# A three-layer block on one core: first attention ordered by token tile, its values held stationary on two column strips, and three conditioning pieces weighed by GpSimd

## The reference

```
# layer_ab (first attention)
y = rms_norm(x, norm_g) @ w_in            # split into qa ka va qi ki wi za qb kb vb zb
oa = attention A: 8 heads of 64, 2 key/value heads, keys chosen by an index score (top 64)
ob = attention B: 8 heads of 64, 2 key/value heads, window of 128 tokens, a sink per head
mix = concatenate([oa * silu(za), ob * silu(zb)])
x = x + mix @ w_out                        # 1024 x 1024
# layer_cd starts with
y = rms_norm(x, norm_g) @ w_in
# conditioning of the third layer: 12 pieces of 512 columns
mod = silu(c) @ w_ada + b_ada              # one row for all tokens
```

## Time and profile before

| | us |
|---|---|
| median of 3 executions | 909.4 (907.77 to 909.72) |
| the profiled execution, its own time | 911.11 |
| its span, first to last instruction | 909.3 |
| granted TensorE clock, mean over the span | 0.949 of full speed (1.00 in every stretch up to 400 us) |

### The profile page before, as it was taken

One profiled execution on the slowest core, in us unless ns is written; L12 is line 12 of the kernel. 1 busy time (PEld: TensorE's weight loads), 2 busy tenths in 40 slices (PEclk: granted clock), 3 DMA queues, 4 the chain that ended last, 5 costly groups with the idle time before them and its releaser, 6 DMA issues.

```text
span 909.3 us, 13058 instructions
## 1 busy us (share of the span) xinstructions
PE 775.5 (85%) x5393; PEld 465.6 (51%) x5393; DVE 373.5 (41%) x885; ACT 168.4 (19%) x473; POOL 40.5 (4%) x36
## 2 busy tenths in 40 slices
PE   7999899999998999999999987858766686677655
PEld 3544664456476644456578573535534444344332
DVE  2478668557854676766441212111111111121113
ACT  3222630223356301041120100000010100001001
POOL 1110000012400000001000000000000000000000
PEclk9999999999999999999999997889899889899888
DMA  9984506765002749987679999999999999999994
GB/s 343 394 291 155 186 1 241 269 231 186 1 1 82 277 130 352 392 338 321 232 269 396 406 425 430 430 430 427 426 427 429 430 428 429 427 428 429 427 428 162
DMA packets 54555, 284.38 MB, mean 313 GB/s; under 512 B 2800, under 2 KB 7280, under 8 KB 41968
## 3 DMA queue, kind: packets, MB, share of 16 engines
q1 hardware_dynamic: 54512, 283.81, 78.0%
HBM read 282.75 MB, written 1.05 MB: 312 GB/s over the span
## 4 chain that ended last, share of the span: by engine, by line
PE 55%; DMA 34%; DVE 5%; issue 2%; ACT 2%; POOL 1%; SPq 1%; DVEq 0%; POOLq 0%
DMA ring<-in_up_w 30%; PE banks L2002 15%; PE banks L1850 9%; PE banks L2413 8%; PE banks L2248 4%; DMA ring<-in_down_w 3%; PE banks L1954 3%; PE banks L2461 2%; PE banks L1882 2%; PE banks L2398 2%; DMA ring<-in_ada_w 1%; PE banks L1929 1%; POOL rs L590 1%; PE banks L1980 1%; PE banks L2492 1%
## 5 line engine op out<-in xcount | busy, mean ns | idle before, releaser
L2413 PE MATMUL banks<-ring,QT 128*32 128x256 f32 x1696 | 143.0, 445 | 56.7 <-DMA ring<-in_up_w 56.7
L2002 PE MATMUL banks<-ring,hT 128*128 128x512 f32 (+4 forms) x384 | 157.9, 566 | 2.4 <-DMA ring<-in_ab_w 2.1
L2413 PEld LDWEIGHTS banks<-ring,QT 128*32 128x32 f32 x1696 | 71.9, 123 | 105.7 <-DMA ring<-in_up_w 44.1
L2002 PEld LDWEIGHTS banks<-ring,hT 128*128 128x128 f32 x384 | 72.4, 193 | 75.5 <-issue 68.6
L1746 DVE TENSOR_TENSOR QT<-banks,MOD 32x256 f32<-32x256 f32 x128 | 53.8, 421 | 138.5 <-PE banks L2461 137.2
L1737 DVE TENSOR_TENSOR QT<-QT,banks 64x256 f32<-64x256 f32 x32 | 13.5, 423 | 191.4 <-ACT QT L943 191.4
L1850 PE MATMUL banks<-ring,hT 128*128 128x512 f32 x192 | 83.9, 594 | 1.9 <-ACT hT L628 1.8
L2461 PE MATMUL banks<-ring,QT 128*32 128x256 f32 x992 | 66.0, 408 | 14.6 <-ACT QT L950 12.4
L590 POOL TENSOR_TENSOR rs<-st,mhalf 128x1 f32<-128x1 f32 (+7 forms) x27 | 33.3, 1237 | 863.3 <-DVE st L1783 451.7
L943 ACT ACTIVATE QT<-banks 64x256 f32<-64x256 f32 x32 | 12.0, 375 | 294.4 <-PE banks L2413 294.4
L1185 DVE SCALAR_TENSOR_TENSOR extra<-ring,cs,extra 128x512 f32<-128x512 f32 x84 | 63.1, 752 | 2.9
(11 more groups left out here) (361 smaller groups left out, 767.6 us busy)
## 6 DMA issues: line engine op xcount, KB each, us to landing
ring<-in_down_w SPq DMA_DIRECT2D x30, 2048.0 KB, 21.8
ring<-in_up_w SPq DMA_DIRECT2D x30, 2048.0 KB, 23.6
ring<-in_gate_w SPq DMA_DIRECT2D x23, 2048.0 KB, 20.4
ring<-in_ada_w SPq DMA_DIRECT2D x12, 2048.0 KB, 15.4
probs<-in_gate_w SPq DMA_DIRECT2D x8, 2048.0 KB, 29.2
ring<-in_ab_w SPq DMA_DIRECT2D x4, 2048.0 KB, 19.4
ring<-in_cd_w SPq DMA_DIRECT2D x4, 2048.0 KB, 13.5
ring<-in_in_w SPq DMA_DIRECT2D x4, 2048.0 KB, 14.5
```

The source lines that it names most:

```text
L2002: ins = pe.matmul(bank[b][:, 0:n], hT[:, k, t * P:(t + 1) * P], w[:, k, :], start=(k == 0), stop=(k == KD - 1))
L2413: return pe.matmul(bank[1][CAP * j:CAP * j + CAP, 0:256], XG[:, k, CAP * s:CAP * s + CAP], wk[:, :, 2 * (j % 2):2 * (j % 2) + 2], start=(k ...
```

## The change

The units of the first attention are ordered by tile: B t0, B t0, A t0, A t0, then the same for t1. The values become the stationary operand: 128 keys x 64 columns on column strips 0 and 64, the turned probabilities of two heads move past them with 256 columns, and the outputs come out transposed, straight as `hT` needs them. So the gates have to be transposed too: VectorE multiplies them by the reciprocal (`scale_gates`), TensorE turns them (`turn_gates`), VectorE copies them into `hT` (`take_gates`) and multiplies by the outputs (`gate_values`). The `abm` transposes and their copies go. The first tile's projection is put inside: (t0, piece 0) ahead of the values of unit 6, (t0, piece 1) ahead of those of unit 7. The two `about` pieces are laid out by head, each in four loads of 64 partitions. GpSimd weighs pieces 1, 2 and 3, in place in the ring slot, between `aaq1` and `cd0`.

```diff
-UNITS = ([("B", g, t) for t in range(NT) for g in range(2)] + [("A", g, t) for t in range(NT) for g in range(2)],
+UNITS = ([(kind, g, t) for t in range(NT) for kind in "BA" for g in range(2)],
...
+        def weighed(c):
+            return ("half", 1 + 11 * c) if c in (1, 2, 3) else ("ada_mm", max(c - 2, 1))
...
-                               ("ada_mm", c + 1)))
+                               weighed(c)))
...
-        add_cols("about", ab_out_w, D, (0, 1))
+        def add_about(c):
+            by_head = ab_out_w.rearrange("(a g r d) n -> a g d r n", a=2, g=2, r=4)
+            chunks.append((f"about{c}", [(2048 * a, 2048, 4, by_head[a, g, :, :, 512 * c:512 * c + 512], g)
+                                         for a in range(2) for g in range(2)], ("about_mm", 3 + c)))
+        add_about(0)
         add_ada(1, 4)
-        add_cols("about", ab_out_w, D, (1, 2))
+        add_about(1)
         add_cd(0)
         add_cd(1)
         add_ada(4, 5)
... (gpsimd)
+            def weigh(c):
+                if c == 1:
+                    pool.wait_ge(*upto("ab_k", 2))
+                if c == 3:
+                    pool.wait_ge(*upto("ada_s", 1))
+                arrived(pool, f"ada{c}")
+                w = weights(f"ada{c}")[:, :].rearrange("p (k n) -> p k n", k=KD)
+                done = 1 + 11 * (c - 1)
+                for k in range(KD):
+                    pool.tensor_scalar(w[:, k, :], w[:, k, :], cs[:, 1, k:k + 1], None, ALU.mult).then_inc(sem("half"), 1)
+                pool.wait_ge(*upto("half", done + 8))
+                pool.tensor_tensor(w[:, 0:4, :], w[:, 0:4, :], w[:, 4:8, :], ALU.add).then_inc(sem("half"), 1)
+                pool.wait_ge(*upto("half", done + 9))
+                pool.tensor_tensor(w[:, 0:2, :], w[:, 0:2, :], w[:, 2:4, :], ALU.add).then_inc(sem("half"), 1)
+                pool.wait_ge(*upto("half", done + 10))
+                pool.tensor_tensor(ada_acc(c), w[:, 0, :], w[:, 1, :], ALU.add).then_inc(sem("half"), 1)
...
+                if name == "aaq1":
+                    pool.wait_ge(*upto("c_e", 1))
+                    for c in range(1, 4):
+                        weigh(c)
... (vector)
+            def scale_gates(u):
+                kind, g, t = ALL_UNITS[u]
+                o = slice(4 * u, 4 * u + 4)
+                v.wait_ge(*upto("exp", 4 * u + 4))
+                if kind == "B":
+                    v.wait_ge(*upto("sinkexp", g + 1 + 2 * t))
+                    link(v.tensor_tensor(sm[:, o], sm[:, o], sk[:, o], ALU.add))
+                link(v.tensor_scalar(sm[:, o], sm[:, o], 1e-30, None, ALU.max))
+                link(v.reciprocal(rc[:, o], sm[:, o]))
+                by = rc[:, o].rearrange("p (g r) -> p r g", g=2).unsqueeze(3).to_broadcast([P, 2, 2, HD])
+                go(v.tensor_tensor(gates_of(kind, g, t), gates_of(kind, g, t), by, ALU.mult), "zr_j")
+            def take_gates(u):
+                v.wait_ge(*upto("zr_T", u + 1))
+                go(v.tensor_copy(gated_rows(*ALL_UNITS[u]), value_bank(u)[:, 256:512].rearrange("p (r n) -> p r n", r=2)), "zr_Tv")
+            def gate_values(u):
+                v.wait_ge(*upto("zr_Tv", u + 1))
+                v.wait_ge(*upto("pv", u + 1))
+                rows_ = gated_rows(*ALL_UNITS[u])
+                link(v.tensor_tensor(rows_, rows_, value_bank(u)[:, 0:256].rearrange("p (r n) -> p r n", r=2), ALU.mult), "post")
...
-            attention(0, before_outputs, lambda u: ada(0) if u == 4 else None, first_gate)
-            weigh(1)
-            turned_rows("abm", 1)
+            max_unit(0)
+            max_unit(1)
+            weigh(0)
+            evacuated(5, 0)
+            for u in range(6):
+                if u == 4:
+                    evacuated(5, 1)
+                scale_gates(u)
+                take_gates(u)
+                max_unit(u + 2)
+                gate_values(u)
+                if u == 3:
+                    ada(0)
+            scale_gates(6)
+            take_gates(6)
+            scale_gates(7)
+            take_gates(7)
+            add_x("about", 0)
+            gate_values(6)
+            gate_values(7)
+            add_x("about", 1)
+            ada(1)
+            scale_x("cd", 0)
+            weigh(4, range(0, 2))
+            turned_rows("cdx", 0, "cd_col")
+            add_x("about", 2)
+            weigh(4, range(2, 4))
+            add_x("about", 3)
+            weigh(4, range(4, 5))
+            scale_x("cd", 1)
+            ada(2)
+            turned_rows("cdx", 1, "cd_col")
+            weigh(4, range(5, 8))
+            ada(3)
             weigh(5)
... (TensorE)
+                    for kb in range(nb):
+                        for j in range(2):
+                            a = AB["va" if kind == "A" else "vb"] + HD * j
+                            ins = pe.matmul(value_bank(u)[HD * j:HD * j + HD, 0:256], Y[:, kb, a:a + HD],
+                                            PTB[:, u % 2, kb, 256 * j:256 * j + 256], start=(kb == 0), stop=(kb == nb - 1))
...
-            attention(0, fill=first_sum, early=last_gate, ahead=lambda: first_outputs(0))
-            project("about", D, first_ready, ada_sums({2: 2}, 2))
+            score_unit(0)
+            score_unit(1)
+            last_gate()
+            for u in range(7):
+                turn_unit(u)
+                turn_gates(u)
+                if u < 6:
+                    score_unit(u + 2)
+                if u == 0:
+                    pe.wait_ge(*upto("abin_Pv", 6))
+                if u == 3:
+                    pe.wait_ge(*upto("share", 1))
+                    ada_sum(0)
+                if u == 6:
+                    project_about(0, 0)
+                    turn_unit(7)
+                    turn_gates(7)
+                unit_values(u)
+            project_about(0, 1)
+            unit_values(7)
+            ada_sum(1)
+            project_about(1, 0)
+            pe.wait_ge(*upto("cd_xn", 1))
+            pe.wait_ge(*upto("ada_v", 2))
+            turn_rows("cdx", 0, 0)
+            project_about(1, 1)
+            rows_copied("cdx", 0)
+            pe.wait_ge(*upto("about_x", 2))
+            project_cd(0, 0, 0)
+            pe.wait_ge(*upto("about_x", 4))
+            ada_sum(2)
+            pe.wait_ge(*upto("cd_xn", 2))
+            turn_rows("cdx", 0, 1)
+            ada_sum(3)
+            rows_copied("cdx", 1)
+            project_cd(0, 1, 1)
+            ada_sum(4)
             project_cd(1, 0, 0)
```

More of the change, by code:

```diff
@@ L116, in build @@
         stages("_mm", [("abin", 12), ("about", 4), ("cdin", 12), ("cdout", 4), ("win", 8), ("wout", 4)])
+        stages("_j", [("zr", 8), ("joined", 8)])
         stages("_Pa", [("abin", 6), ("cdin", 6), ("win", 4)])
@@ L438, in _ @@
                     sp.wait_ge(*upto(s, n))
-                for off, n, k, src in parts:
-                    dst = ring[i % SLOTS][:, off:off + n].rearrange("p (k n) -> p k n", k=k)
+                for off, n, k, src, *half in parts:
+                    rows_ = slice(64 * half[0], 64 * half[0] + 64) if half else slice(0, P)
+                    dst = ring[i % SLOTS][rows_, off:off + n].rearrange("p (k n) -> p k n", k=k)
                     sp.dma_start(dst, src).then_inc(sem(f"slot{i % SLOTS}"), 16)
@@ L764, in _ @@
             for t in range(NT):
-                turned_rows("abm", t)
-            for t in range(NT):
-                act.wait_ge(*upto("about_x", 3 + t))
+                act.wait_ge(*upto("about_x", 2 + 2 * t))
                 squares_of_x("cd", t)
@@ L1033, in add_x @@
                 product = part(0, 512)[:, 0, :] if tag == "wout" else tmp[:, :]
-                c, t = j // 2, j % 2
+                c, t = (j % 2, j // 2) if tag == "about" else (j // 2, j % 2)
                 cols = slice(512 * c, 512 * c + 512)
@@ L1134, in both @@
                     return Y[:, t, a:a + 512].rearrange("p (g n) -> p g n", g=2)[:, :, 128 * g:128 * g + 128]
-                if kind in "AB":
-                    z = both(AB["za" if kind == "A" else "zb"])
-                    link(v.tensor_tensor(z, z, got, ALU.mult), "post")
-                elif kind == "S":
+                if kind == "S":
                     link(v.tensor_tensor(both(0), both(0), got, ALU.add), "post")
@@ L1897, in value @@
             def value(kind, g, h, kb):
-                if kind in "AB":
-                    a = AB["va" if kind == "A" else "vb"] + 64 * (h // 2)
-                    return Y[:, kb, a:a + 128]
                 if kind in "SW":
@@ L1931, in turn_unit, with turn_gates @@
                 ins.then_inc(sem("pT"), 1)
+            def turn_gates(u):
+                kind, g, t = ALL_UNITS[u]
+                if u > 1:
+                    pe.wait_ge(*upto("post", u - 1))
+                pe.wait_ge(*upto("zr_j", u + 1))
+                a = AB["za0" if kind == "A" else "zb0"] + 256 * g
+                for r in range(2):
+                    ins = pe.transpose(value_bank(u)[:, 256 + P * r:384 + P * r], Y[:, t, a + P * r:a + P * r + P], ident)
```

(34 more changed lines are left out.)

74 lines of the change are left out of this document (32 added, 42 removed).

## The result

The changed kernel takes 950.17 us (median of 4, 948.51 to 952.34) where the kernel before takes 908.87 on the same chip: a ratio of 1.0457, 95% interval 1.0432 to 1.0482, so 4.6% slower. The forecast was 944.0, inside a range of 914 to 960. The profiled execution has a span of 947.9 against 909.3.

A forecast was written before the change was run, and what follows sets the result against it. TensorE held 55% of the chain of waits, transfers 34%, VectorE 5%; in the attention no engine was full. Order 8.7 plus GpSimd's 11.8, 6.9 and 7.4 made 34.8 on 911.1, less 1.7 for the median: 944, range 914 to 960.

The forecast's parts named there:

- the case held likeliest: Attention and input stage: GpSimd's weighing holds up VectorE, 34.8 us slower in sum; chance 0.76, of which 0.05 above 960.
- Order, +8.7 forecast: Up to the second cd projection's start (the mark): new order's longer attention and later load of ada4, +8.7 us.
- ring: Attention, once per unit: gates turned, scores, maximum, small operations, values, next gates scaled, product; six turns, together 29.5 us.
- rival of strips in turn: Attention values: the two column strips run one after the other instead of overlapping, +2.2 us on top; no separate chance.
- GpSimd, +26.1 forecast: VectorE held up by GpSimd's weighing of pieces 1, 2 and 3: 11.8, 6.9 and 7.4 us.
- The one-input product, 0.7: GpSimd's scaling of 512 columns in the weighing: 0.7 us, taken between VectorE's 0.48 and GpSimd's 1.33.
- Piece 1, 11.8: From 73.3: VectorE's eleven products alternate with GpSimd's instructions, each behind one, 11.8 us late.
- the first maximum near 108: Sign of VectorE being held up: its first maximum near 108, where it was at 87.9.
- Piece 2, 6.9: From 92.3, beside the top-8 rounds: the three operations behind them meet GpSimd's three additions, 6.9 us.
- Piece 3, 7.4: Units 4 and 5: some eight small operations wait 0.7 each, additions fall partly into waits, 7.4 us of 13.4.
- VectorE isn't held up: Rival for GpSimd beside VectorE: one-input streaming leaves room, or only additions hold; +8.7, 918 us; chance 0.11.
- TensorE sets the pace: Rival for the attention: it costs TensorE's sum of 43.0 us, mark at 172.2, -3.9, or 905.5 us; chance 0.10.

The follow-up runs named there:

- e6: Changed kernel with the new order kept, but VectorE instead of GpSimd weighs pieces 1, 2 and 3: 919.8 us.
- e5: Kernel before, in its own order, with GpSimd instead of VectorE weighing pieces 1, 2 and 3: 927.1 us.
- e3: Changed kernel without GpSimd's scalings of pieces 1, 2 and 3, their three additions a piece kept: 946.0 us.
- e1: Changed kernel with GpSimd's eleven instructions per piece cut to one scaling of one row: 925.3 us.
- e12: Changed kernel with 49 matmuls added on TensorE, results overwritten, where it waits for the gates: 963.2 us.
- e8: e7 with the scores of unit u+2 issued ahead of the turning of unit u's gates on TensorE: 907.8 us.
- e9: e8 with unit 0's gates scaled ahead of weighing piece 0, and piece 0's sum and addition one turn earlier: 904.9 us.
- e7: e6 with piece 4's first five weighing instructions moved behind the copy of the turned rows and the scaling of x: 912.5 us.
- e2: Changed kernel with GpSimd's eight scalings a piece kept and the three additions of pieces 1, 2 and 3 removed: 928.4 us.

## Why the prediction was right, and where its steps failed

**Sign and size** came out: 944.0 forecast, 950.2 measured, by the case held likeliest (VectorE held up by GpSimd, and the order slower by itself). Two marks split the shift of 38.9. e6 against before is the order: +11.5 at the mark. The changed kernel against e6 is GpSimd: +27.4. Forecast were 8.7 and 26.1. By the medians the two parts are 10.6 and 30.7.

**Order, +8.7 forecast, +11.5.** The mechanisms are shown: ring, third projection, load and idle time each within about 1 us in e6. Missing is the clock, which the prediction took to be full. It costs 2.3 in `project_cd(0, 0)` and is most of the 1.2 by which the fourth turn is longer (scores and masks at 110.38 take 1.50 and 1.03 instead of 1.13 and 0.60, the sum behind them 1.91 instead of 1.02). That is a term left out, not one mis-sized.

**Strips.** They overlap: a unit of two blocks takes 1.08 us for eight instructions where e5, with the old form, shows 1.95 for sixteen. The rival of strips in turn falls. But on the chain (start, time, what) the values take 1.01, not the forecast 0.86, and the projection behind them 7.06 instead of 6.87:

```profile
164.00 1.01 PE banks L2025 x8
165.02 7.06 PE banks L2171 x16
```

In e6 the chain shows the same, and the sum behind the other strips at 1.06 instead of 0.86: 0.7 us in all behind the ring. The prediction put the draining of TensorE at nothing, since it had no price for it; whether these 0.7 are that, no run separates. What it cites of the Trainium skill on this stands in "TensorEngine Tiling (Array Packing)" under Key Properties, not under Restrictions.

**GpSimd, +26.1 forecast, +27.4**, is near in its sum and wrong in most of its parts, so a good part of the agreement is luck: two errors cancel, a scaling priced at less than half and a hold by scalings that is hardly there. The prediction's own ends, +34.8 at 0.7 and +49 at 1.33, continued to the 1.65 measured give an estimate of +56, or 965, above its range.

- *The one-input product, 0.7*, is 1.65, outside the bounds of 0.48 and 1.33. The upper bound, a product with two inputs, was no bound.
- *Piece 1, 11.8: "they alternate with GpSimd's, each behind one".* This step failed for scalings: of VectorE's first six operations with two inputs three took 1.06 to 1.11, three kept 0.69 or 0.41. For additions it is right, as e3 shows, where the same six alternate with six additions (4.91, 2.72, 1.64, then 4.73, 2.56, 1.64). Until the first of the top-8 rounds VectorE lost 2.0 us. By the turn of the first gates it was 7.6 later than in e6, 8.4 counted from the first scores. The rest are piece 1's additions, which met the three operations behind the rounds (6.0 us instead of 1.0), and 1.2 beside piece 0. The sign "the first maximum near 108" doesn't follow from the prediction's own term: 87.9 + 11.8 is 99.7. Measured was 93.37.
- *Piece 2, 6.9.* Near in size, wrong in place: the longer scalings moved its additions into the ring, where the first turn took 10.8 instead of 3.8; some 1.0 of these 7.0 are gates, scores and masks at the lower clock (2.4 us from the gates to VectorE's maximum, in e6 1.4).
- *Piece 3, 7.4.* The last turn took 11.7 instead of 4.8. The prediction had small operations held by scalings, some eight times 0.7. It was the additions: two operations of four columns took 4.22 and 2.07 where they need 0.17, a product 1.35 instead of 0.42.

So what holds VectorE is the addition, not "streaming like the first kind". The earlier trace rows showed two-input GpSimd work alone; from it the prediction concluded on one-input work, and e1 to e3 part them: 3.1 us for the scalings, 20.7 for the additions. The rival "VectorE isn't held up" had named this very case, "only the additions hold", but priced it at nothing (+8.7, 918): its condition came true, its time didn't.

**The clock inside the ring.** Between 104.71 and 153.15 TensorE is busy 27.9 us, in the ring of e6 22.7 for the same 142 instructions. So at most 5.3 us of the ring's growth of 18.1 are slow matmuls. The third and fourth turns (7.05 and 8.7 where e6 has 5.4 and 7.6) and the second (5.0, 3.7) hold no addition, and exceed e6's by 4.1 together. In the fourth some 0.4 are VectorE's, whose operations take up to 0.55 beside the scalings of piece 3. The rest, 3.7 us, is argued to be the clock's, and was not measured by itself, since e12 missed its size.

**Rival "TensorE sets the pace", 905.5.** It named as its conditions a VectorE free of GpSimd and hidden handovers. e8 and e9 come near its time, 907.8 and 904.9, but not by its way. It had the third projection end at 139.2; in e9 it ends at 147.7, since TensorE still waits in the ring (busy 19.9 of 25.8 us). What they gain instead is the idle time ahead of `project_cd(0, 0)`, which the rival kept and e7's order removed. So no run reached TensorE's own pace in the attention.

## What to carry to other kernels

Moving work to an engine that is idle costs what it does to its neighbour: price it by the kind of instruction, and look where its long two-input instructions fall: here operations of four columns on the chain took 3.5 and 4.2 us beside an addition of 2048. TensorE, when it had waited some microseconds, paid again behind the wait, by the lower clock (7.2 us and 2.3 more in e6); so put first, on every queue, what TensorE waits for next. When a reorder loses, look at the order inside its ring before giving it up: here the weighing back on VectorE and three edits of order, a few lines each, took the same change from +41 to -5 us.

## What was not expected of the hardware

- GpSimd scales 512 fp32 columns by a factor per partition in 1.65 us, but adds two inputs of 512 columns in 1.26. "GPSIMD Engine Reference" (Performance versus the Vector engine) in the Trainium skill gives 0.77 as the best case for a loop over 512 elements; the trace shows more than twice that for this operation.
- Beside GpSimd's scalings VectorE's two-input products take about 0.4 us more, and 4-column operations at times 0.1 to 0.5 more (0.45 to 0.54 instead of 0.17 in e2). Beside its additions both kinds wait to the end, except a reciprocal of four columns (0.18). A maximum over PSUM (0.69), top-8 rounds (0.43) and products with one input in PSUM (0.41) kept their durations beside both.
- TensorE's granted clock, 1.00 in the whole attention before, stood at its lower level behind waits of 4.6, 6.3 and 7.6 us for VectorE (0.71 on average over the ring), fell in e6 behind one of 2.25 us too, and came back with TensorE kept busy. In the ring of e8, with no wait above 2.10 us, it stayed at 1.00.
